# The last piece of each stage finished tile by tile, transposes set among the next matmuls, gates moved by DMA

## What is computed

```python
h_l = x * (1.0 + s1) + sh1                       # s1, sh1, g1: rows of 1024, from the conditioning
y_l = _chunk_gmlp(h_l, ...)                      # layer 0; layer 1: _retention_mixer
x = _layernorm(DN_ALPHA * x + g1 * y_l, ln1_g[i], ln1_b[i])
x = _layernorm(DN_ALPHA * x + g2 * _sq_relu_mlp(x * (1.0 + s2) + sh2, w1, w2), ln2_g[i], ln2_b[i])
# layer 0: the same for ctx, with its own s, sh, g; layer 1 returns the latents alone
```

## Time and profile before

| | before |
|---|---|
| median of 3 runs | 2095.38 us (2094.12 to 2095.62) |
| profiled execution, own time | 2095.84 us |
| span of its trace | 2094.0 us |
| PE busy | 2041.5 us, 97% of the span |
| DVE, ACT, POOL busy | 1044.8, 599.1, 507.1 us |
| mean granted PE clock | 0.992 |

### The profile page before, as it was taken

The page is one execution under the profiler, slowest core; times in us unless marked ns, Lnnn a source line. Parts: engine busy times, 40 slices in busy tenths (PEclk is TensorE's granted clock), DMA queues, the critical chain, the costliest instruction groups (busy, mean ns, idle before and its releaser), DMA issues.

```text
span 2094.0 us, 27570 instructions
## 1 busy us (share of the span) xinstructions
PE 2041.5 (97%) x9932; PEld 1714.5 (82%) x9932; DVE 1044.8 (50%) x1527; ACT 599.1 (29%) x856; POOL 507.1 (24%) x381
## 2 busy tenths in 40 slices
PE   6999999999999999999999999999999989999996
PEld 3778899898888888888878888888888867888884
DVE  3335555559433433344484544554553576445546
ACT  2222222225122222221253223323323342332231
POOL 0300203327520331133260020020020037223323
PEclk9999999999999999999999999999999999999998
DMA  9742111133223323333222122221221212332321
GB/s 373 270 166 70 61 61 51 61 111 101 93 98 118 112 87 99 115 107 119 75 66 71 61 86 61 70 86 55 76 76 61 71 61 92 99 98 92 120 92 58
DMA packets 58035, 204.16 MB, mean 97 GB/s; under 512 B 6640, under 2 KB 7024, under 8 KB 57840
## 3 DMA queue, kind: packets, MB, share of 16 engines
q1 hardware_dynamic: 57104, 199.96, 28.2%
q10 hardware_dynamic: 864, 3.28, 0.5%
HBM read 201.12 MB, written 2.10 MB: 97 GB/s over the span
## 4 chain that ended last, share of the span: by engine, by line
PE 88%; issue 5%; POOL 2%; DVE 2%; ACT 1%; DMA 1%; SPq 0%; DVEq 0%; POOLq 0%; ACTq 0%
PE bank L554 28%; PE bank L555 28%; PE bank L556 28%; PE bank L664 2%; POOL res_lat L1605 2%; PE bank L750 1%; DMA mod<-mod_units_d 1%; POOL res_ctx L1605 0%; DVE w_lo L1125 0%; DVE bst L1177 0%; PE bank L807 0%; DVE gy L1232 0%; POOL rstd L1595 0%; DVE res_lat L1287 0%; DVE rbuf L1214 0%
## 5 line engine op out<-in xcount | busy, mean ns | idle before, releaser
L1125 DVE TENSOR_TENSOR w_lo<-raw,w_hi 128x1024 fp32r<-128x1024 f32 x256 | 342.6, 1338 | 424.2 <-ACT w_hi L855 423.4
L855 ACT ACTIVATE w_hi<-raw 128x1024 fp32r<-128x1024 f32 x256 | 270.3, 1056 | 726.4 <-PE bank L556 725.7
L1605 POOL TENSOR_TENSOR res_lat<-res_lat,gy 128x512 f32<-128x512 f32 x192 | 264.0, 1406 | 869.4 <-DVE gy L1232 860.1
L554 PE MATMUL bank<-hT_hi,w_hi 128*128 128x384 f32 (+2 forms) x1216 | 429.8, 353 | 6.0 <-DVE hT_lo L1218 4.4
L555 PE MATMUL bank<-hT_lo,w_hi 128*128 128x384 f32 (+2 forms) x1216 | 425.3, 350 | 0.0
L556 PE MATMUL bank<-hT_hi,w_lo 128*128 128x384 f32 (+2 forms) x1216 | 425.3, 350 | 0.0
L554 PEld LDWEIGHTS bank<-hT_hi,w_hi 128*128 128x128 f32 x1216 | 229.2, 188 | 38.3 <-issue 14.8
L554 PE MATMUL bank<-w_hi,hT_hi 128*128 128x512 f32 x640 | 252.6, 395 | 4.6 <-DVE hT_lo L1134 4.6
L555 PE MATMUL bank<-w_lo,hT_hi 128*128 128x512 f32 x640 | 250.3, 391 | 0.0
L556 PE MATMUL bank<-w_hi,hT_lo 128*128 128x512 f32 x640 | 250.1, 391 | 0.0
L555 PEld LDWEIGHTS bank<-hT_lo,w_hi 128*128 128x128 f32 x1216 | 229.2, 188 | 15.8 <-issue 0.2
(11 more groups left out here) (150 smaller groups left out, 2426.3 us busy)
## 6 DMA issues: line engine op xcount, KB each, us to landing
raw<-w_units_d SPq DMA_DIRECT2D x256, 512.0 KB, 3.4
mod<-mod_units_d SPq DMA_DIRECT2D x48, 512.0 KB, 8.2
mod<-mod_units_d SPq DMA_DIRECT2D x64, 384.0 KB, 3.7
lnbc<-ln_d SPq DMA_DIRECT2D x8, 512.0 KB, 5.4
xT<-xT_d SPq DMA_DIRECT2D x4, 768.0 KB, 14.0
dec<-dist_d ACTq DMA_DIRECT2D x4, 768.0 KB, 4.2
res_lat<-x_d SPq DMA_DIRECT2D x1, 2048.0 KB, 14.3
out_d<-res_lat SPq DMA_DIRECT2D x4, 512.0 KB, 3.2
```

The source lines that it names most:

```text
L554: nc.tensor.matmul(out, s_hi, m_hi, start=first, stop=False)
L855: nc.scalar.activation(w_hi[:, slot(phase, k), :], raw[:, s, :], ACT.Copy).then_inc(hi_done, 1)
L1125: tt(w_lo[:, w, :], raw[:, s, :], f32(w_hi[:, w, :]), ALU.subtract).then_inc(lo_done, 1)
L1605: gt(r, r, gy[:, e % 2, :], ALU.add).then_inc(res_added, 1)
```

## The change

- **Tile by tile.** The last pieces are phases of their own (`gmlpz`, `ffn0z`, `headz`, `ffn1z`). PE sweeps the first quarter of `down` over the latent tiles, then finishes tile after tile, both halves; DVE drains, and takes statistics, in that order. In `headz` the order is 3, 2, 1, 0, and `transpose_y(0)` stands behind the sweep. The last three units of such a piece have halves of their own (`xw0`, `xw1`), and are split ahead, as no slot has to come free. In `ffn1z` gain, offset and store go by tile too, all on DVE; the last tile's offset and store go in two halves.
- **Transposes.** Only four column blocks of the latents are transposed ahead; the rest stand between matmuls of the next stage's first unit (`ln_between`). For ffn1 the two first units go together, 256 tokens at a time (`first_units`), with the second 16 transposes in between.
- **Gates.** The diagonals, the 24 matmuls and ACT's copies go. SP stores the columns of `modc` as a row in HBM (`store_gate`, 1024 elements of 4 bytes each, 6 such stores) and loads it broadcast to 128 partitions (`load_gate`).
- Line numbers of the changed kernel are higher: L1299 is the split L1125, L1601 the normalise of the values L1393, L1430 the drain L1232, L1478 and L1483 gain and offset, L620 to L622 the three products, L808 the transposes.

```diff
...
+LN_ORDER = {"ln0a": list(range(TILES0)), "ln0b": list(range(TILES0)), "ln1a": [3, 2, 1, 0], "ln1b": [0, 1, 2, 3]}
+LN_ACT = {"ln0a": 4, "ln0b": 4, "ln1a": 3}
...
+        XW = {"gmlpz": (xw0_hi, xw0_lo), "ffn0z": (xw0_hi, xw0_lo), "headz": (xw1_hi, xw1_lo), "ffn1z": (xw1_hi, xw1_lo)}
+        def halves_of(phase, k):
+            n = k - (PER[phase]["units"] - 3)
+            if phase in XW and 0 <= n < 3:
+                return [x[:, n, :] for x in XW[phase]]
+            s = (BASE[phase]["units"] + k) % SPL
+            return w_hi[:, s, :], w_lo[:, s, :]
...
+            def store_gate(r, layer, part, groups):
+                for v in range(groups):
+                    sp.dma_start(rows_d[r, v, :].rearrange("(j p) -> p j", p=P),
+                                 modc[:, layer, 8 * part:8 * part + 8, v], allow_slow_non_contiguous=True)                        .then_inc(rows_out, 16)
+            def load_gate(r, groups):
+                for v in range(groups):
+                    g = (gate_lat, gate_ctx)[v]
+                    sp.dma_start(g[:, :], rows_d[r, v, :].partition_broadcast(P)).then_inc(gate_in, 16)
...
+            sp.wait_ge(dve_drain, drained("v", 2, "cols0")[1])
+            store_gate(0, 0, 2, 2)
+            store_gate(1, 0, 5, 2)
+            sp.wait_ge(rows_out, 64)
+            load_gate(0, 2)
...
+            def down_blocks(phase, k0, order, a_hi, a_lo, ready, late=None):
+                banks = dict((x[0], x[1]) for x in STEPS[phase])
+                seen = set()
+                def part(t, half, q):
...
+                sweep = [t for t in order if t < LAT]
+                if late:
+                    sweep, final = sweep[:-1], sweep[-1]
+                for t in sweep:
+                    last = part(t, 0, 0)
+                if late:
+                    late()
+                elif len(order) == LAT:
+                    last.then_inc(pe_step, 1)
+                for n, t in enumerate(order):
+                    if t >= LAT:
+                        last = part(t, 0, 0)
+                        if t == order[-1]:
+                            last.then_inc(pe_step, 1)
+                    part(t, 0, 1).then_inc(pe_step, 1)
+                    last = part(t, 1, 0)
+                    if t == order[-1]:
+                        last.then_inc(pe_step, 1)
+                    part(t, 1, 1).then_inc(pe_step, 1)
+                    if late and n == 0:
+                        part(final, 0, 0).then_inc(pe_step, 1)
...
-            def gates(phase, n):
-                for j in range(n):
-                    free(phase, 0, f"gate{j}")
-                    pe.wait_ge(diag_ready, diags[0] + 1)
-                    b = dict((x[0], x[1]) for x in STEPS[phase])[f"gate{j}"]
-                    nc.tensor.matmul(bank[b][:, :], ones[:, :], DIAG[j], start=True, stop=True).then_inc(pe_step, 1)
...
+            def ln_between(phase):
+                return {2: lambda: ln(phase, 0, (4, 5)), 4: lambda: ln(phase, 0, (6, 7)),
+                        6: lambda: ln(phase, 1, range(KC))}
...
+            def first_units():
+                for k in range(2):
+                    pe.wait_ge(lo_done, before("units", "ffn1") + (k + 1))
+                for g, (t0, t1) in enumerate(LN_GROUPS["ln1a"]):
+                    a, b = t0 * P, t1 * P
+                    for kc in range(KC):
+                        if (g, kc) == (0, 4):
+                            ln("ln1a", 1, range(KC))
+                        pe.wait_ge(stage_lo, before("stage", "ln1a") + KC * g + kc + 1)
+                        c = slice(kc * P, (kc + 1) * P)
+                        for k in range(2):
+                            if g == kc == 0:
+                                free("ffn1", 0, f"up{k}.0")
+                            hi, lo = halves_of("ffn1", k)
+                            last = mm3(bank[4 + k][:, a:b], hi[:, c], lo[:, c], hT_hi[:, kc, a:b], hT_lo[:, kc, a:b],
+                                       g == kc == 0, g == 1 and kc == KC - 1)
+                            if (g, kc) == (1, KC - 1):
+                                last.then_inc(pe_step, 1)
...
+                for n, t in enumerate(LN_ORDER[phase][:LN_ACT[phase]]):
+                    act.wait_ge(nbias_ready, NB_BASE[phase] + n + 1)
...
+            def down_blocks(phase, ln_phase, before_last, next_phase):
+                order = LN_ORDER[ln_phase]
+                drain_block(phase, 0, order)
+                drain_block(phase, 1, order)
+                for n in range(1, len(order)):
+                    first_half(phase, n - 1, order)
+                    drain_block(phase, 2 * n, order)
+                    second_half(phase, n - 1, ln_phase)
+                    negative_bias(ln_phase, n - 1)
+                    if n == before_last:
+                        split_lo(next_phase, 0, 0)
+                        if phase == "headz":
+                            split_lo(next_phase, 0, 1)
+                    if n - 1 >= LN_ACT[ln_phase]:
+                        normalise(ln_phase, n - 1)
+                    drain_block(phase, 2 * n + 1, order)
+                first_half(phase, len(order) - 1, order)
...
+                drain_block(phase, 0, order)
+                drain_block(phase, 1, order)
+                for n in range(1, LAT):
+                    first_half(phase, n - 1, order)
+                    drain_block(phase, 2 * n, order)
+                    second_half(phase, n - 1, "ln1b")
+                    gain(n - 1)
+                    drain_block(phase, 2 * n + 1, order)
+                    if n < LAT - 1:
+                        shift(n - 1, slice(0, D))
+                n = LAT - 1
+                e = BASE[phase]["add"] + 2 * n + 1
+                dve.wait_ge(dve_drain, drained(phase, 0, f"down1.{n}")[1])
+                r = res(n)[:, 512:1024]
+                tt(r, r, gy[:, e % 2, :], ALU.add).then_inc(last_added, 1)
+                first_half(phase, n, order)
+                dve.wait_ge(last_added, 1)
+                statistics([r], n, BASE_STAT["ln1b"] + n, 1)
+                gain(n)
+                shift(n - 1, slice(0, D))
+                shift(n, slice(0, 512))
+                shift(n, slice(512, D))
...
+            dve.wait_ge(gate_in, 32)
...
+            ln_split("ln1a", {0: lambda: second_half("headz", 3, "ln1a"), 1: lambda: normalise("ln1a", 3)})
...
```

More of the change, by code:

```diff
@@ L416, in build @@
         }
+        for p, z in (("gmlp", "gmlpz"), ("ffn0", "ffn0z"), ("heads", "headz"), ("ffn1", "ffn1z")):
+            UNIT_END[z] = UNIT_END[p][:-3]
         block = keep.enter_context(nc.Block())
@@ L570, in feature_unit @@
                         c = slice(kc * P, (kc + 1) * P)
-                        last = mm3(out, w_hi[:, s, c], w_lo[:, s, c], hT_hi[:, kc, a:b], hT_lo[:, kc, a:b],
+                        last = mm3(out, hi[:, c], lo[:, c], hT_hi[:, kc, a:b], hT_lo[:, kc, a:b],
                                    kc == 0, kc == KC - 1)
@@ new lines, in _ @@
+            for h in range(HEADS - 1):
+                head("heads", h, h)
+            head("headz", 0, HEADS - 1)
+            ln("ln1a", 0, range(KC))
+            def first_units():
[15 more added lines that the diff above has]
+                            if (g, kc) == (1, KC - 1):
+                                last.then_inc(pe_step, 1)
@@ L845, in _ @@
+            ffn1("ffn1", 0, True)
+            with nc.tensor.Fori(1, PIECES_F - 1) as p:
+                ffn1("ffn1", p)
+            ffn1("ffn1z", 0)
         @block.scalar
@@ L1435, in ffn @@
                         split_lo(phase, i, c + 1)
+                    if c == CH - 1 and phase in XW:
+                        for k in range(CH + 1, 2 * CH):
+                            split_lo(phase, i, k)
                     for g in range(groups):
```

691 lines of the change are left out of this document (375 added, 316 removed).

## The result

The changed kernel takes 2099.18 us (median of 18 runs, 2097.49 to 2101.84) where the one before takes 2095.29 (18 runs): ratio 1.0021, interval 1.0013 to 1.0028. One execution of the kernel before took 6686.56 us; its other 17 lie between 2093.92 and 2096.37. The changed kernel is slower by 3.9 us; the forecast was 2082.8 with a range up to 2095.0. The profiled execution spans 2099.0 us, against 2094.0.

The account below looks back on a forecast made before the run. PE, busy 97% of the span, was taken as the bound, with losses at stage ends and the way into the gMLP. Terms 0 - 3.4 - 3.9 + 0.3 - 6.0 = -13.0 against 2095.84 gave 2082.8 us, range 2076.3 to 2095.

Parts of the forecast that it names:

- The wait at the gates: First term, way into the gMLP: eight matmuls leave PE, unit 1's split waits for gate loads; 0, from -2.25 to +10.
- rival (c): Way into the gMLP: stores hold DVE and PE for tens of microseconds, from 100 ns per element; 2105.2 us, chance 0.11.
- 256p: Gate stores: 256 single elements on each of 16 DMA engines at price p; 20 ns each taken, 5.1 us.
- (b): Way into the gMLP: elements cost 50 ns, +7.4 us, and PE's clock returns late, +2.2; 2092.4 us, chance 0.12.
- Out of the gMLP: Window behind the gMLP: eight gate matmuls go, PE's waits stay 3.1 us in all; -3.4 us.
- Out of ffn0: Window behind ffn0: ACT's first pair starts earlier, a split precedes its groups, an idle wait goes; -3.9 us.
- the ring: Found afterwards, not forecast: ACT feeds DVE, DVE feeds PE's products, and the products hold back ACT's next input.
- Out of the heads: Window from the heads to ffn1's third unit: 27.4 us against 27.16; +0.3, ends -2 and +2.5.
- The new fault: Start of ffn1: two first units end together, so the third unit's slot comes free only then; wait about 6 us.
- The last end: Behind PE's last product: tile order shortens DVE's remaining work, 20.5 us becomes 14.5; -6.0, ends -4.5 and -8.
- Rival (d): Last pieces: DVE, not PE, sets the pace, so the ends bring 4 us instead of 13; 2091.8 us, chance 0.12.

Follow-up runs that it names:

- the gates alone: Kernel before with gates moved to DMA alone, the first wait late, stage ends as before: 2092.34 us, ratio 0.9985.
- the transposes earlier: Changed kernel with DVE's gate wait moved to the first drain, and column blocks 4 to 7 transposed earlier among the first products: 2079.43 us, ratio 0.9931.
- the late wait: Changed kernel with DVE waiting for the first gate rows only ahead of its first drain of the gMLP: 2082.42 us, ratio 0.9938.

## Why the prediction was wrong, step by step

**The wait at the gates: the term that failed.** The mechanism was named, in the term and in rival (c): stores of single elements, and all of DVE behind a wait that it doesn't need yet. What failed is the size: 256p plus 1.7 us, at p = 20 ns, gave a result of 0; the stretch measured +15.1 us. Both parts were too small. For the way of a small transfer I had 1.7 us, from one load of 8 KB, and it was 10: 0.9 from the issue to the first packet, 9.1 behind the last. For 256p I had 5.1, and it was 10 as well, of which the first half of the packets took 2 and the second 8. The nearest rows were of a load in longer packets, and few of them; what a long queue of single elements does to its own packets, and what passes behind the last, no row showed.

So the price came out between my rivals (b), +7.4, and (c), +20.2, and the time between theirs. That (b)'s 12.8 us for 256p is near the 10 measured is luck: it took 50 ns for every packet, and the trace has 7.5 and 112. (c) was the right rival in kind; its chance of 0.11 was too low for a term for which no row existed, and the range left it out.

The Trainium skill's rule in "DMA: Bandwidth & Descriptors", section "Rules for kernel authors" (a non-contiguous last dimension is one descriptor per element; make it contiguous), was the one to follow: single elements took 10.4 us here, the same 4 KB in a row 1.2. The figure of about 10.5 ns per packet in the same page of the Trainium skill, section "Measured", is of the size of the fast half of the packets here (7.5), and would have misled in the same way as my row did.

With that wait moved, the way into the gMLP gained 2.5 us, where I had -2.25 as the best case.

**Out of the gMLP: -3.4 forecast, -2.2 measured.** The reason given, eight matmuls off PE's path, is refuted for the order before by the gates alone, which gave 0. I had read that PE's busy time was there, and not what followed it: PE waited 0.7 us behind them, for ACT. So the gain that did come goes with the order tile by tile, under which ACT begins its first pair 1.1 us behind the last product (I had 3.95); the new order with the gates still on PE was not run. It was cut by a step that I had put at no cost, "the transposes are not fewer, they stand elsewhere": PE waited 4.2 us (18.96 less 14.74), not 3.1.

**Out of ffn0: -3.9 forecast, -1.1 measured.** I let ACT's eight pairs run back to back from their start. They started earlier than I thought (1.1 us behind the last product), but were held up for 3.70 us by the ring. I also had written that this end's idling, and its low clock, go: there is a wait of 2.61 us in place of one of 2.43, and the mean clock is 0.93 in both. With the transposes earlier it is 21.4, nearer to my 20.6. A part stays unforecast: beside a DVE operation POOL's power took 1.53 us, not 0.55, and DVE's normalise of a context tile waits for it, 0.44 us. POOL, then DVE, from the end of the gMLP, where it is the same:

```profile
484.93 0.55 POOL L1819 TENSOR_TENSOR rstd<-veps,tiny 128x1 f32<-128x1 f32 x1
...
490.37 1.53 POOL L1819 TENSOR_TENSOR rstd<-veps,tiny 128x1 f32<-128x1 f32 x1
...
489.99 1.50 DVE L1299 TENSOR_TENSOR w_lo<-raw,w_hi 128x1024 fp32r<-128x1024 f32 x1
491.94 0.81 DVE L1448 TENSOR_SCALAR res_ctx<-res_ctx,mv,rstd 128x1024 f32<-128x1024 f32 x1 [0.44 <-POOL rstd L1819]
```

**Out of the heads: +0.3 forecast.** -0.7 in the window and +1.2 behind it, where PE's clock is low. The new fault was there as described: 5.75 us of wait for the third unit (I had about 6), behind 3.9 us for the first block (3.3).

**The last end: -6.0 forecast, -7.6 measured.** Right in mechanism. I had allowed 1.5 us for collisions with POOL, and DVE loses next to nothing by them. DVE's last gain and offsets, then POOL beside that gain:

```profile
2092.12 1.28 DVE L1478 SCALAR_TENSOR_TENSOR res_lat<-res_lat,mv,lnbc 128x1024 f32<-128x1024 f32 x1
2093.32 2.60 DVE L1483 SCALAR_TENSOR_TENSOR res_lat<-res_lat,rstd,lnbc 128x1024 f32<-128x1024 f32 x3
...
2092.29 1.52 POOL L1819 TENSOR_TENSOR rstd<-veps,tiny 128x1 f32<-128x1 f32 x1 [2.63 <-DVE veps L1360]
```

The gain takes 1.28 us and each offset no more than its share of 2.60, where one took 3.36 beside POOL before. The collision is still there, but it is POOL that pays: its power takes 1.52 us, not 0.55, and DVE, which has another tile's offset to do first, doesn't wait for it. The Trainium skill, "SBUF — State Buffer", section "SBUF: two separate sides", has it that of such a pair of operations the one that starts first gets the shared ports for its whole length, and the other waits; the rows agree, as the gain began at 2092.12, the power at 2092.29.

**The sum.** Rival (d) is out: the four ends brought 11.6 us, not 4. Without the first term I had -13.0; the late wait came to -13.0. That is no confirmation: it is made of -2.5 for a term of 0, -3.9 for terms of -7.0 in the windows of the first three ends, +1.3 in the rest of ffn1, and -7.6 for -6.0. Errors of 1 to 3 us cancelled.

## What to carry to other kernels

Put a new wait at the first instruction that reads what it waits for, not at the head of the phase: here that is the difference between 4 us slower and 13 us faster. Instructions that fill an engine's wait can cost nothing (the gates alone: eight matmuls out, 0 us at that end), so before counting them as a gain, look at what their engine waits for next. Where work is moved among instructions that wait, ask who feeds those: transposes behind products that wait for ACT's and DVE's results made ACT wait for PE.

## What was not expected of the hardware

- A store whose elements go out singly (4 bytes each) landed 10.4 and 10.9 us after issue for 1024 elements, 10.9 and 11.2 for 2048, 20.1 and 19.3 for 4096; the same 4 KB from one partition as one row, 1.2. Nearly all packets in the trace end 8 to 9 us before the landing. Of 4096 elements the first half moves in 2 us, at 7 to 8 ns of an engine's time each, the second is drawn out over 8 us, at about 112. Near 1036 us, beside weight loads, two such stores took 15.7 us each in the median.
- Two sizes, 11.2 and 20.1 us, fitted a price per element exactly and were explained wrongly by it; the third size, 10.4, showed it.
- A POOL power of 0.55 us took 1.53 beside a DVE subtraction on SBUF. The subtraction took 1.50 in place of 1.22; it had begun at 489.99, with POOL's add of 489.12 still running until 490.41.
- A wait of PE of 2.20 us ahead of the fifth unit of ffn1 made the next product take 0.66 us, not 0.39; with the gate matmuls gone from the order before, a wait of 4.12 left 28 transposes at a mean of 0.55; a wait of 2.61 behind the gMLP left the clock at 1.00, one of 2.61 behind ffn0 did not (0.93).
